# Pairs of recurrence chunks in one product per level, keys carried in the exponent, and channel sums added on VectorE

## What is computed

```python
u = causal_depthwise_conv(u, conv_w[l], conv_b[l])
u = jax.nn.silu(layernorm(u, conv_ln_g[l], conv_ln_b[l]))
y_conv = (u @ w_conv_pw[l]) * jax.nn.silu(cv_gate)
```

```python
b = jnp.cumsum(ln, axis=2)
inter = jnp.einsum('bhcd,bhde->bhce', qn * jnp.exp(b), S)
diff = b[:, :, :, None, :] - b[:, :, None, :, :]
decay = jnp.exp(jnp.where(tril[None, None, :, :, None], diff, -jnp.inf))
A = jnp.einsum('bhtd,bhtsd,bhsd->bhts', qn, decay, kn)
intra = jnp.einsum('bhts,bhse->bhte', A, vn)
k_dec = kn * jnp.exp(b_last[:, :, None, :] - b)
S_new = jnp.exp(b_last)[..., None] * S + jnp.einsum('bhsd,bhse->bhde', k_dec, vn)
```

## Time and profile before

| | us |
|---|---|
| median of 3 runs (1950.12 to 1951.86) | 1950.2 |
| profiled execution, whole time | 1952.02 |
| profiled execution, span from first to last instruction | 1950.0 |
| mean granted TensorE clock | 0.997 |

### The profile page before, as it was taken

One profiled execution on the slowest core, in us unless ns is written; L12 is line 12 of the kernel. 1 busy time (PEld: TensorE's weight loads), 2 busy tenths in 40 slices (PEclk: granted clock), 3 DMA queues, 4 the chain that ended last, 5 costly groups with the idle time before them and its releaser, 6 DMA issues.

```text
span 1950.0 us, 25600 instructions
## 1 busy us (share of the span) xinstructions
PE 1923.9 (99%) x8958; PEld 1570.7 (81%) x8958; DVE 1113.0 (57%) x1505; ACT 789.3 (40%) x1086; POOL 242.0 (12%) x209
## 2 busy tenths in 40 slices
PE   8999999999999999999999999999999999999999
PEld 6898888888888767887788888888888888887887
DVE  6664567777777667777534444334455455546332
ACT  6433423333333463234533334345555555654111
POOL 3500000000000003443100000001222222220000
PEclk9999999999999999999999999999999999999999
DMA  7344144444444326764122222222121122123441
GB/s 270 108 133 190 66 159 168 170 172 172 172 172 171 109 86 226 248 236 159 68 89 89 89 89 77 77 87 82 70 86 70 73 72 86 65 87 119 140 151 65
DMA packets 50406, 244.66 MB, mean 125 GB/s; under 512 B 5688, under 2 KB 6968, under 8 KB 29760
## 3 DMA queue, kind: packets, MB, share of 16 engines
q1 hardware_dynamic: 49920, 240.99, 34.9%
q10 hardware_dynamic: 448, 3.17, 0.4%
HBM read 235.72 MB, written 8.41 MB: 125 GB/s over the span
## 4 chain that ended last, share of the span: by engine, by line
PE 93%; DVE 4%; ACT 2%; issue 1%; DMA 0%; POOL 0%; DVEq 0%; SPq 0%; ACTq 0%
PE ps_p L535 27%; PE ps_p L537 26%; PE ps_p L536 26%; PE ps_s L799 3%; PE ps_s L617 2%; PE ps_o L635 2%; PE ps_t L625 1%; PE ps_x L554 1%; DVE act_lo L1762 1%; ACT w_hi L872 0%; DVE w_lo L1279 0%; PE ps_s L588 0%; PE ps_s L589 0%; PE ps_t L588 0%; PE ps_t L590 0%
## 5 line engine op out<-in xcount | busy, mean ns | idle before, releaser
L535 PE MATMUL ps_p<-act_hi,w_hi 128*128 128x512 f32 x2288 | 930.6, 407 | 6.2 <-DVE w_lo L1279 2.5
L537 PE MATMUL ps_p<-act_hi,w_lo 128*128 128x512 f32 x2288 | 893.8, 391 | 0.0
L536 PE MATMUL ps_p<-act_lo,w_hi 128*128 128x512 f32 x2288 | 892.7, 390 | 0.0
L535 PEld LDWEIGHTS ps_p<-act_hi,w_hi 128*128 128x128 f32 x2288 | 430.6, 188 | 96.8 <-issue 6.9
L537 PEld LDWEIGHTS ps_p<-act_hi,w_lo 128*128 128x128 f32 x2288 | 429.8, 188 | 92.5
L536 PEld LDWEIGHTS ps_p<-act_lo,w_hi 128*128 128x128 f32 x2288 | 431.0, 188 | 88.2 <-issue 5.3
L872 ACT ACTIVATE w_hi<-raw 128x2048 fp32r<-128x2048 f32 x154 | 294.4, 1912 | 424.9 <-PE ps_p L537 413.5
L1279 DVE TENSOR_TENSOR w_lo<-raw,w_hi 128x2048 fp32r<-128x2048 f32 x154 | 361.8, 2349 | 146.0 <-ACT w_hi L872 136.0
L1537 DVE CUSTOM_DVE_ANT_0 mkv<-mkv,c_all 128x1024 f32<-128x1024 f32 x96 | 146.2, 1559 | 0.2 <-DVE hcol L1665 0.2
L1930 POOL TENSOR_TENSOR ssq_a<-ssq_a,wk 128x512 f32<-128x512 f32 x15 | 37.3, 2486 | 751.0 <-ACT wk L1114 751.0
L1024 ACT ACTIVATE tp<-tp,stat 128x128 f32<-128x128 f32 (+1 forms) x64 | 36.0, 563 | 169.8 <-DVE stat L1514 169.8
(11 more groups left out here) (270 smaller groups left out, 1770.7 us busy)
## 6 DMA issues: line engine op xcount, KB each, us to landing
raw<-wt_dram SPq DMA_DIRECT2D x156, 1024.0 KB, 4.8
mkv<-ada_dram SPq DMA_DIRECT2D x96, 512.0 KB, 4.7
qkv<-xT_dram SPq DMA_DIRECT2D x16, 256.0 KB, 2.8
spill_dram<-Y SPq DMA_DIRECT2D x16, 256.0 KB, 2.2
hqk<-spill_dram SPq DMA_DIRECT2D x16, 256.0 KB, 2.7
out_dram<-wk SPq DMA_DIRECT2D x16, 256.0 KB, 2.0
Y<-xT_dram SPq DMA_DIRECT2D x3, 1024.0 KB, 9.9
mem_raw<-memT_dram SPq DMA_DIRECT2D x4, 512.0 KB, 10.3
```

Of the source, the lines that this page charges most:

```text
L535: mm(o, wh, hi[:, k, 0:n], start=at == 0, stop=False)
L536: mm(o, wh, lo[:, k, 0:n], start=False, stop=False)
L537: last = mm(o, wl, hi[:, k, 0:n], start=False, stop=at == KT - 1)
```

## The change

For levels 1 to 7 a chunk is now multiplied with its neighbour. In `hz` the left halves of every chunk hold the decayed keys; the right halves of an even chunk hold the queries of the odd chunk of its pair, and those of the odd chunk the queries of the even one. One product of the pair (128 columns) then gives the scores of the even chunk and, transposed, those of the odd one. Two products a level take the place of four. They are gathered in `hP`; at the head's end its upper triangles are copied into `hA`, and `turn_pairs` (two transposes on TensorE) gives those of the odd chunks.

The keys are no longer multiplied in: `hbk` is b plus the negative logarithm of the keys, so the exponential of the difference is the decayed key itself. ScalarE writes it into `hz` (left halves), and takes the exponential of the right halves in `hd`, without Abs; GpSimd multiplies the queries only, in two instructions of another access pattern. `diff` is in two halves of 128x256. The factor 1 - lb moves from the keys to the query. `hkd` comes from ScalarE. The levels' hooks move forward. Before level 3 and later ScalarE, no longer GpSimd, waits until `hz` is free.

In the gate phase the four channel tiles are added on VectorE (three adds, `channels_added`) into `wk[:, 3]`, and TensorE sums the result with one product. The first sum moves from hook 3 to hook 7. `conv_gate` is cut into `conv_z` and the rest, and the splits for gate 3 and out1 move relative to these; `conv_gate(2)` goes into the middle of the `y_hi` and `y_lo` of out1.

The diff, without declarations of semaphores and without unchanged lines:

```diff
@@ -191,6 +192,9 @@
+hP = mkv[:, 0, 0, :].rearrange("p (t n) -> p t n", t=2)
+hbk = mkv[:, 0, 2:4, :].rearrange("p a m -> p (a m)")
@@ -363,6 +370,15 @@
+def left_halves(ap, h):
+    return blocks(ap, 2 * h)[:, :, 0:h]
+def chunk_halves(ap, parity, h):
+    pairs = ap.rearrange("p (a c b n) -> p c a b n", c=2, a=QT // 2, n=2 * h)
+    return pairs[:, parity, :, :, h:2 * h]
@@ -695,11 +711,9 @@
-            for c in range(NCONV):
-                last = mm(ps_x[:, :], ones, (Y[:, c, :], qkv[:, c, :])[k], start=c == 0, stop=c == NCONV - 1)
-            return last
+            return mm(ps_x[:, :], ones, wk[:, 3, :], start=True, stop=True)
...
-    project("gate", 0, 0, hooks={3: channel_sum(0)})
+    project("gate", 0, 0, hooks={7: channel_sum(0)})
@@ -785,23 +799,29 @@
-                    pe.wait_ge(level_in.sem, level_in.at("hg", i, n + 1))
-                    left = right = hz[:, (n - 1) % 2, :]
+                    pe.wait_ge(level_in.sem, level_in.at("hg", i, n))
+                    z = hz[:, (n - 1) % 2, :]
+                    for t in range(0, QT, 2):
+                        last = mm(ps_s[:, n % 2, t * P // 2:(t + 2) * P // 2], z[:, t * P:(t + 1) * P],
+                                  z[:, (t + 1) * P:(t + 2) * P], start=True, stop=True, skip_group_check=True)
...
-                    left, right = hk, hq
-                for t in range(QT):
-                    c = slice(t * P, (t + 1) * P)
-                    moving, o = (right[:, c], ps_s[:, 0, c]) if n == 0 else (
-                        right_halves(right[:, c], HALVES[n - 1]),
-                        blocks(ps_s[:, n % 2, t * P // 2:(t + 1) * P // 2], HALVES[n - 1]))
-                    last = mm(o, left[:, c], moving, start=True, stop=True, skip_group_check=True)
+                    for t in range(QT):
+                        c = slice(t * P, (t + 1) * P)
+                        last = mm(ps_s[:, 0, c], hk[:, c], hq[:, c], start=True, stop=True,
+                                  skip_group_check=True)
...
+        def turn_pairs():
+            pe.wait_ge(scores_free.sem, scores_free.at("hg", i, NLEV))
+            for t in range(QT // 2):
+                last = pe.transpose(ps_s[:, 0, t * P:(t + 1) * P], hP[:, t, :], ident)
+            last.then_inc(pair_turned.sem, 1)
...
-            pe.wait_ge(level_in.sem, level_in.at("hg", i, 1))
+            pe.wait_ge(level_exps.sem, level_exps.at("hg", i, 1))
@@ -838,10 +858,10 @@
-        project("hg", i, 2, hooks={10: level(0), 12: level(1), 14: level(2)})
-        project("hg", i, 3, hooks={0: level(3), 2: level(4), 4: level(5), 6: level(6), 8: level(7),
-                                   9: lambda: turn_value("hg", i, 1, hvT[:, :], QT),
-                                   11: chunk_states, 13: within, 15: across},
+        project("hg", i, 2, hooks={9: level(0), 11: level(1), 12: level(2), 14: level(3)})
+        project("hg", i, 3, hooks={0: level(4), 2: level(5), 4: level(6), 6: level(7),
+                                   7: lambda: turn_value("hg", i, 1, hvT[:, :], QT),
+                                   9: chunk_states, 10: turn_pairs, 13: within, 15: across},
@@ -1065,11 +1085,7 @@
-        e = fn(qkv[:, c, :], Y[:, c, :], ACT.Square)
-        if c < NCONV - 1:
-            o.step(e)
-        else:
-            e.then_inc(side_in.sem, 1)
+        fn(qkv[:, c, :], Y[:, c, :], ACT.Square).then_inc(ln_squares, 1)
@@ -1084,11 +1100,10 @@
+    split("gate", 0, 2)
...
-    split("gate", 0, 2)
...
-    conv_gate(2)
@@ -1096,6 +1111,8 @@
+        if k == 10:
+            conv_gate(2)
@@ -1211,10 +1228,14 @@
-            if n:
-                o.step(fn(d, d, ACT.Abs))
-                o.settle()
-            fn(d, d, ACT.Exp, scale=-1.0).then_inc(level_exps.sem, 1)
+            if n == 0:
+                fn(hkd[:, :], d, ACT.Exp, scale=-1.0).then_inc(level_exps.sem, 1)
+                return
+            h = HALVES[n - 1]
+            if n >= 3:
+                act.wait_ge(scores_full.sem, scores_full.at("hg", i, n - 1))
+            o.step(fn(left_halves(hz[:, (n - 1) % 2, :], h), left_halves(d, h), ACT.Exp, scale=-1.0))
+            fn(right_halves(d, h), right_halves(d, h), ACT.Exp).then_inc(level_exps.sem, 1)
@@ -1586,14 +1607,24 @@
-    def conv_gate(j):
+    def conv_z(j):
...
+    def conv_gate(j):
...
-    dve.sem_inc(side_in.sem, 1)
+    def channels_added(c4):
+        o.step(tt(wk[:, 3, :], c4[:, 0, :], c4[:, 1, :], ALU.add))
+        o.settle()
+        o.step(tt(wk[:, 3, :], wk[:, 3, :], c4[:, 2, :], ALU.add))
+        o.settle()
+        tt(wk[:, 3, :], wk[:, 3, :], c4[:, 3, :], ALU.add).then_inc(side_in.sem, 1)
+    dve.wait_ge(heads_done.sem, heads_done.at("fox", 7, 1))
+    channels_added(Y)
@@ -1602,6 +1633,9 @@
+    dve.wait_ge(ln_squares, NCONV)
+    channels_added(qkv)
+    conv_z(0)
@@ -1623,13 +1657,14 @@
+    conv_z(1)
+    split("gate", 0, 2)
...
-    split("gate", 0, 2)
...
+    conv_z(2)
...
-    conv_gate(2)
@@ -1639,7 +1674,10 @@
-    y_lo(range(4, KT))
+    y_lo(range(4, 10))
+    conv_gate(2)
+    y_lo(range(10, KT))
+    conv_z(3)
@@ -1754,6 +1792,7 @@
+    do(dve.memset(hP[:, :, :], 0.0))
@@ -1792,27 +1831,33 @@
-        dve.wait_ge(gate_sig.sem, gate_sig.at("hg", i, 1))
-        do(ts(hk, hk, hcol[:, 1, bass.ds(i, 1)], None, ALU.mult))
...
+        do(tt(hbk, hb[:, :], wk[:, 1, :], ALU.add))
...
-            width, ref = (HCHUNK, HCHUNK - 1) if n == 0 else (2 * HALVES[n - 1], HALVES[n - 1] - 1)
-            if n >= 2:
-                dve.wait_ge(level_in.sem, level_in.at("hg", i, n - 1))
-            b = blocks(hb[:, :], width)
-            r = b[:, :, ref:ref + 1].broadcast_to([P, S // width, width])
-            tt(blocks(hd[:, n % 2, :], width), b, r, ALU.subtract).then_inc(level_diff.sem, 1)
+            d = hd[:, n % 2, :]
+            if n == 0:
+                r = blocks(hb[:, :], HCHUNK)[:, :, HCHUNK - 1:HCHUNK].broadcast_to([P, NCH, HCHUNK])
+                tt(blocks(d, HCHUNK), blocks(hbk, HCHUNK), r, ALU.subtract).then_inc(level_diff.sem, 1)
+                return
+            if n == 2:
+                dve.wait_ge(level_exps.sem, level_exps.at("hg", i, 1))
+            elif n > 2:
+                dve.wait_ge(level_in.sem, level_in.at("hg", i, n - 2))
+            h = HALVES[n - 1]
+            r = blocks(hb[:, :], 2 * h)[:, :, h - 1:h].broadcast_to([P, S // (2 * h), h])
+            o.step(tt(left_halves(d, h), left_halves(hbk, h), r, ALU.subtract))
+            tt(right_halves(d, h), right_halves(hb[:, :], h), r, ALU.subtract).then_inc(level_diff.sem, 1)
...
-        o.step(tt(hq[:, :], ps_p[:, s, :], wk[:, 3, :], ALU.mult))
+        o.step(stt(hq[:, :], ps_p[:, s, :], hcol[:, 1, bass.ds(i, 1)], wk[:, 3, :], ALU.mult, ALU.mult))
@@ -1824,13 +1869,11 @@
-                h = HALVES[n - 1]
-                a, mask = right_halves(a, h), right_halves(mask, h)
-                b = ps_s[:, n % 2, 0:S // 2].rearrange("p (t b n) -> p t b n", t=QT, n=h)
+                a, b = hP[:, :, :], ps_s[:, n % 2, 0:S // 2].rearrange("p (t n) -> p t n", t=QT // 2)
...
+        diff(3)
...
-        diff(3)
@@ -1840,6 +1883,15 @@
+        a = hA[:, :, :].rearrange("p (a c) n -> p c a n", c=2)
+        tri = upper.broadcast_to([P, QT // 2, P])
+        o.note()
+        o.settle()
+        dve.copy_predicated(a[:, 0], tri, hP[:, :, :])
+        dve.wait_ge(pair_turned.sem, pair_turned.at("hg", i, 1))
+        o.note()
+        o.settle()
+        do(dve.copy_predicated(a[:, 1], tri, ps_s[:, 0, 0:S // 2].rearrange("p (t n) -> p t n", t=QT // 2)))
@@ -1940,29 +1992,19 @@
-        for n in range(NLEV):
+        pool.wait_ge(query_ready.sem, query_ready.at("hg", i, 1))
+        for n in range(1, NLEV):
...
-            if n == 0:
-                pool.wait_ge(side_full.sem, side_full.at("hg", i, 0))
-                o.step(tt(hkd[:, :], hk[:, :], hd[:, 0, :], ALU.mult))
-                o.settle()
-                pool.sem_inc(level_in.sem, 1)
-                pool.wait_ge(query_ready.sem, query_ready.at("hg", i, 1))
-                continue
...
-            if n >= 3:
-                pool.wait_ge(scores_full.sem, scores_full.at("hg", i, n - 1))
-            z = hz[:, (n - 1) % 2, :].rearrange("p (b n) -> p b n", n=2 * h)
-            d = hd[:, n % 2, :].rearrange("p (b n) -> p b n", n=2 * h)
-            k = hk[:, :].rearrange("p (b n) -> p b n", n=2 * h)
-            q = hq[:, :].rearrange("p (b n) -> p b n", n=2 * h)
-            o.step(tt(z[:, :, 0:h], k[:, :, 0:h], d[:, :, 0:h], ALU.mult))
-            tt(z[:, :, h:2 * h], q[:, :, h:2 * h], d[:, :, h:2 * h], ALU.mult).then_inc(level_in.sem, 1)
+            z, d = hz[:, (n - 1) % 2, :], hd[:, n % 2, :]
+            o.step(tt(chunk_halves(z, 1, h), chunk_halves(hq, 0, h), chunk_halves(d, 0, h), ALU.mult))
+            tt(chunk_halves(z, 0, h), chunk_halves(hq, 1, h), chunk_halves(d, 1, h), ALU.mult).then_inc(
+                level_in.sem, 1)
...
-    pool.wait_ge(level_in.sem, level_in.at("hg", 7, NLEV))
```

(6 more changed lines are left out.)

10 lines of the change are left out of this document (7 added, 3 removed).

## The result

| | before | after |
|---|---|---|
| median of 4 runs | 1950.34 (1950.12 to 1951.86) | 1925.68 (1924.9 to 1928.19) |
| profiled execution: time, span | 1952.02, 1950.0 | 1928.19, 1926.4 |
| mean granted TensorE clock | 0.997 | 0.996 |

The ratio is 0.987, with a 95% interval of 0.9859 to 0.9882: 24.7 us faster. The forecast was 1931.3, so 18.9 faster. The profiled execution lies 2.5 above its median, so the spans differ by 1.1 less than the medians do.

What follows compares the result with a forecast made beforehand. TensorE was taken as the bound (busy 1923.9 of 1950.0 us). Eight heads at -1.9 each (15.2) and the gate phase's 3.65 sum to 18.9 off a median of 1950.2: 1931.3, range 1921 to 1944.

Steps and rivals of the forecast that it cites:

- rival A: The forecast itself: products halve, level 3 stands about 1.1 us a head, the rest is met; 1926 to 1937, chance 0.55.
- (1): Recurrence levels: two products of 128 columns for four of 64 cost 0.44 us, not 0.89; gain 3.1 a head.
- (2): Recurrence head's end: turn_pairs adds two transposes on TensorE, 0.22 us a head.
- (3): Recurrence: turn_keys no longer waits for GpSimd's product after ScalarE's exponential; gain 0.2 us a head.
- (4): Recurrence: work moves among the other engines; level 3 comes late by 1.1 us a head, levels 4 to 7 cost 0.1.
- allowance of 0.1 for levels 4 to 7: Recurrence: 0.1 us a head counted for collisions of VectorE's diffs with GpSimd's products; ends 0 and 1.2.
- rival C: Recurrence: the loop of levels 3 to 7 bounds, VectorE's halves and GpSimd's products colliding; 1937 to 1947, chance 0.19.
- (5) to (8): Gate phase and out1: cheaper channel sums, new waits for adds, splits and gates reordered; pointwise product 3.65 us earlier.
- B: Recurrence: all levels met because GpSimd gets its products in ahead of the split; 1923, chance 0.16.
- D: Recurrence: GpSimd's new access pattern costs more, so the kernel gets slower; 1965 at 1.3 us an instruction, chance 0.07.
- E: Recurrence: a block of four records with 128 columns costs 0.89 us after all; heads gain nothing, about 1947, chance 0.03.
- wrong if the heads are under 52.5: Recurrence: sign against the forecast of 53.3 us a head; heads under 52.5 would mean the levels are all met.

Runs made afterwards that it cites:

- four_halves: The changed kernel with each pair product issued as two products of 64 columns, so eight records a level again: 1946.06 us (ratio 0.9973 to the kernel before).
- products_twice: The changed kernel with both GpSimd products of each level issued, awaited and issued again: 1946.39 us (ratio 0.9971 to the kernel before).
- sum_hook9: The changed kernel with the first channel sum behind step 9 in place of 7 of gate tile 0: 1924.99 us (ratio 0.9861 to the kernel before).
- gate_split_early: The changed kernel with the split for gate 3 issued ahead of ln_silu((0, 1)) on ScalarE and VectorE: 1924.28 us (ratio 0.9859 to the kernel before).
- change_again: The changed kernel, unaltered, timed and profiled again on a third occasion: 1925.46 us (ratio 0.9865 to the kernel before).
- split_before: The changed kernel with the heads' weight split issued ahead of masked(0) on VectorE, not behind diff(4): 1920.62 us (ratio 0.9843 to the kernel before).

## Why the prediction was right

The time, 1925.7, is 5.6 below the forecast and inside the range; it lies just under rival A's own (1926 to 1937), with A's mechanism in the trace. Point by point:

**(1) Products.** 0.44 a level and 3.1 a head, as taken. `four_halves` shows that the records make the cost.

**(2), (3) turn_pairs and turn_keys.** 0.22 was forecast and 0.22 read in the timeline (1475.37 - 1474.92 - 0.23). The stall ahead of turn_keys is gone; it was 0.2, as taken (0.23 by starts).

**(4) The calendar of the levels.** Wanted 6.9, 9.2, 10.3 and 12.1; found 6.94, 9.21, 10.34 and 12.17. The split was to end at t = 11.9 and ended at 11.96. The collision is there, at level 3 alone, and it costs every head. Its price is the term that was mis-sized: 1.1 forecast, 0.58 measured. The prediction gave a level two GpSimd instructions of 128x256 with 0.73 each. But each instruction now handles only the right halves of the two chunks of one parity (`chunk_halves`), a quarter of the tile: 128x128, with 0.45 each. I had carried the old instructions' size over and not counted the elements. The product beside the split ended 0.33 after it where I took 0.6, the second lasted 0.45 where I took 0.7: these two are the 0.5 too much in each head. On TensorE's path the stand costs 0.70, with the dearer level behind it. By the Trainium skill ("SBUF — State Buffer", section "Who interferes with whom"), the blocked product would have taken its full 0.45 behind the split. Here it ended 0.33 behind it by the records, so the rule names the right pair of instructions and is 0.1 too dear.

A term was left out as well: the stand of 0.18 that level 3 already had before, which is gone into the new one. The terms of the head as measured: -3.15 + 0.22 - 0.23 - 0.18 + 0.70 = -2.64, and a head lost 2.63. The allowance of 0.1 for levels 4 to 7 was not needed: no wait there in the list. VectorE's halves do meet GpSimd's products (0.66 in place of 0.43 at 1463.13), as rival C had it, but with GpSimd at 0.9 to 1.1 a level the loop has room. `products_twice` takes the room away, and several levels wait.

**(5) to (8) The gate phase.** Forecast -3.65, measured -4.3. The points of the prediction are compared from the first matmul, which it took at 661.25 (the trace has 661.14) and which is at 661.75 in the profile of after: tile 0 ends at 12.8 (forecast 12.8), tile 1 at 25.4 (25.7), gate 3 starts at 38.5 (39.0), the pointwise product at 59.1 (59.65). The waits by starts (for the first 668.14 - 667.07 - 0.23) are 0.84, 0.76, 2.20, 0.32 and 1.46, where 1.0, 1.1, 2.35, 0.4 and 1.75 were forecast: each there, each a little shorter. That the wait for the split stays and only comes earlier was the forecast's main reading, and `sum_hook9` (a shorter wait changes nothing at gate 3) and `gate_split_early` (removing it moves the stand to the low parts) show it, and so does the stretch of 1.2 GHz in `change_again`: the chain sets this part.

**The rivals.** B (1923) has the number nearest to the result but not the cause: it had the levels all met, and 3.5 us of waits say otherwise. What B describes is `split_before`, whose heads have no wait. D and E did not come. The check "wrong if the heads are under 52.5" stood at 52.66, close enough that the size alone would not have told A from B; the row of the wait does. That the total came within 5.6 is in part luck: the stand at level 3 was forecast at 1.1 with instructions of twice their size, and half of it was not there.

**The sum.** 18.9 was forecast and 24.7 measured by the medians. The heads gave 5.8 more than the 15.2 taken (8 x 2.63 = 21.0), the gate phase 0.7 more, and the medians differ by 0.6 less than these two stages do. Of the 5.8, 3.2 is the stand at level 3 (eight times 1.1 - 0.70), 1.4 the old stand that wasn't counted (eight times 0.18), 0.8 the allowance for the later levels, and 0.6 the rounding of the products and of turn_keys (3.15 for 3.1, 0.23 for 0.2). These make 6.0, 0.2 too much.
